# Reordering the work lists of the SSD scan groups (one tile's convolution, two products, and a separate list for the last group)

## The reference, cut to what matters

```
xbc = silu(dwconv_centred(xbc, conv_w, conv_b))          # per group: B, C and four x tiles
cb = einsum('bclgn,bcsgn->bgcls', cc, bc)
wmat = cb[:, :, None] * _segsum_exp(a_cum)               # scores of a chunk
y_diag = einsum('bghcls,bcsghp->bclghp', wmat, xd)       # product inside the chunk
states = einsum('bclgn,bclghp->cbghpn', bc, xd * decay)  # state of each chunk
y_off = einsum('bclgn,cbghpn->bclghp', cc, h_prev) * decay_out
y = rmsnorm((y_diag + y_off + xs * d_skip) * silu(z), gnorm_w);  out = y @ w_out
```

## Time and profile before

| | us |
|---|---|
| median of 3 runs (lowest, highest) | 1253.02 (1252.13, 1253.27) |
| profiled execution: its own time | 1253.8 |
| its span, first to last instruction | 1252.1 |
| TensorE busy in the span | 1154.5 (92%) |
| VectorE busy | 876.2 (70%) |
| ScalarE busy | 616.6 (49%) |
| granted TensorE clock, mean | 0.973 |

### The profile page before, as it was taken

One profiled execution on the slowest core, in us unless ns is written; L12 is line 12 of the kernel. 1 busy time (PEld: TensorE's weight loads), 2 busy tenths in 40 slices (PEclk: granted clock), 3 DMA queues, 4 the chain that ended last, 5 costly groups with the idle time before them and its releaser, 6 DMA issues.

```text
span 1252.1 us, 20419 instructions
## 1 busy us (share of the span) xinstructions
PE 1154.5 (92%) x7420; PEld 693.7 (55%) x7420; DVE 876.2 (70%) x1385; ACT 616.6 (49%) x1100; POOL 86.8 (7%) x102
## 2 busy tenths in 40 slices
PE   3999899998987999899999999997898996999996
PEld 2545444454444447644444444475555585888886
DVE  5695877768677976677878779735466767655654
ACT  4676565656566433633333332225454464566642
POOL 0004013040320000000000000000000000000000
PEclk9999999999997999899999999999999998999998
DMA  9423130221313253246464636421322114355552
GB/s 387 160 76 127 68 135 33 81 86 67 135 68 136 77 216 143 81 176 233 175 233 175 230 135 242 170 98 68 119 75 76 61 42 168 135 201 201 193 187 91
DMA packets 24535, 174.07 MB, mean 139 GB/s; under 512 B 2720, under 2 KB 2720, under 8 KB 5536
## 3 DMA queue, kind: packets, MB, share of 16 engines
q1 hardware_dynamic: 18432, 128.24, 28.2%
q0 software_dynamic: 4608, 33.56, 7.5%
q10 hardware_dynamic: 1440, 11.53, 2.5%
HBM read 172.27 MB, written 1.05 MB: 138 GB/s over the span
## 4 chain that ended last, share of the span: by engine, by line
PE 77%; DVE 12%; ACT 6%; issue 4%; DMA 1%; DVEq 0%; ACTq 0%; SPq 0%
PE bank L1726 21%; PE bank L1728 20%; PE bank L1727 20%; ACT wh L428 2%; PE bank L1900 2%; DVE wl L963 2%; DVE sq L1142 1%; PE bank L2175 1%; PE bank L1930 1%; PE bank L2189 1%; PE bank L1941 1%; ACT arena L535 1%; PE bank L1915 1%; ACT arena L470 1%; DVE arena L1225 1%
## 5 line engine op out<-in xcount | busy, mean ns | idle before, releaser
L1726 PE MATMUL bank<-hh,wh 128*128 128x512 f16 (+1 forms) x1168 | 396.7, 340 | 13.9 <-DVE hl L1032 5.3
L1727 PE MATMUL bank<-hl,wh 128*128 128x512 f16 (+1 forms) x1168 | 396.2, 339 | 0.0
L1728 PE MATMUL bank<-hh,wl 128*128 128x512 f16 (+1 forms) x1168 | 396.0, 339 | 0.0
L963 DVE SCALAR_TENSOR_TENSOR wl<-raw,wh 128x1024 f16<-128x1024 f32 x224 | 270.2, 1221 | 176.1 <-ACT wh L428 174.5
L428 ACT ACTIVATE wh<-raw 128x1024 f16<-128x1024 f32 x224 | 229.0, 1041 | 252.6 <-PE bank L1728 203.5
L1726 PE MATMUL bank<-arena,wh 128*128 128x256 f16 (+1 forms) x620 | 194.2, 313 | 6.8 <-DVE arena L1472 2.8
L1728 PE MATMUL bank<-arena,wl 128*128 128x256 f16 (+1 forms) x620 | 194.0, 313 | 0.0
L1727 PE MATMUL bank<-arena,wh 128*128 128x256 f16 (+1 forms) x620 | 194.0, 313 | 0.0
L1726 PEld LDWEIGHTS bank<-hh,wh 128*128 128x128 f16 x1168 | 115.7, 99 | 114.4 <-issue 30.9
L1728 PEld LDWEIGHTS bank<-hh,wl 128*128 128x128 f16 x1168 | 115.5, 99 | 89.0 <-issue 2.7
L1727 PEld LDWEIGHTS bank<-hl,wh 128*128 128x128 f16 x1168 | 115.5, 99 | 81.4 <-issue 10.0
(11 more groups left out here) (261 smaller groups left out, 1336.9 us busy)
## 6 DMA issues: line engine op xcount, KB each, us to landing
raw<-wgu SPq DMA_DIRECT2D x44, 1024.0 KB, 4.7
arena<-wadaT POOLq DMA_DIRECT2D x32, 1024.0 KB, 5.0
raw<-wdn SPq DMA_DIRECT2D x16, 896.0 KB, 4.8
raw<-wxg SPq DMA_DIRECT2D x12, 1024.0 KB, 5.0
arena<-wada SPq DMA_DIRECT2D x8, 1024.0 KB, 19.2
raw<-wz SPq DMA_DIRECT2D x8, 1024.0 KB, 4.7
araw<-wada ACTq DMA_DIRECT2D x8, 1024.0 KB, 4.8
raw<-wout SPq DMA_DIRECT2D x8, 1024.0 KB, 5.9
```

The lines of the kernel that those rows point to most:

```text
L963: ve.scalar_tensor_tensor(wl[:, u.slot, a:b], raw[:, u.slot, a:b], WS, wh[:, u.slot, a:b], ALU.mult, ALU.subtract).then_inc(lo_done, 1)
L1726: pe.matmul(o, wh[:, u.slot, wsl], ahi[:, k, a:e], start=st, stop=False)
L1727: pe.matmul(o, wh[:, u.slot, wsl], alo[:, k, a:e], start=False, stop=False)
L1728: i = pe.matmul(o, wl[:, u.slot, wsl], ahi[:, k, a:e], start=False, stop=en)
```

## The change

```diff
@@ ScalarE
+            def silu_ahead():
+                act.activation(small[:, 60:61], eps, ACT.Silu)
@@ group(g, u)
                 tap(g + 1, 3)
+                exps(g, 2, 0)
+                exps(g, 2, 1)
                 cvt(u.plus(3))
-                for q in range(4):
-                    exps(g, 2, q)
+                exps(g, 2, 2)
+                exps(g, 2, 3)
                 silu_xbc(g + 1, 0)
                 silu_xbc(g + 1, 1)
-                silu_xbc(g + 1, 2)
-                silu_xbc(g + 1, 3)
                 evac_pre(u.plus(2), g + 1, 4, 0)
                 evac_pre(u.plus(2), g + 1, 5, 1)
                 tap(g + 1, 4)
                 tap(g + 1, 5)
+                exps(g, 3, 0)
+                exps(g, 3, 1)
                 cvt(u.plus(4))
-                for q in range(4):
-                    exps(g, 3, q)
+                exps(g, 3, 2)
+                exps(g, 3, 3)
+                silu_xbc(g + 1, 2)
+                silu_xbc(g + 1, 3)
                 silu_xbc(g + 1, 4)
@@ last_group(g, u), from square_z(0) on
                 square_z(0)
+                silu_ahead()
                 z_out(u)
                 ada_parts(g)
                 act.dma_start(araw[:, :], crow).then_inc(crow_in, 16)
                 cvt(u.plus(2))
-                square_z(1)
                 for q in range(4):
                     exps(g, 1, q)
-                for q in range(3):
-                    exps(g, 2, q)
+                square_z(1)
+                exps(g, 2, 0)
+                exps(g, 2, 1)
                 act.wait_ge(gl_ok, 2)
+                silu_ahead()
                 z_out(u.plus(1))
+                exps(g, 2, 2)
+                exps(g, 2, 3)
                 square_z(2)
                 cvt(u.plus(3))
-                exps(g, 2, 3)
+                for q in range(3):
+                    exps(g, 3, q)
                 square_z(3)
-                exps(g, 3, 0)
-                exps(g, 3, 1)
+                exps(g, 3, 3)
                 act.wait_ge(gl_ok, 4)
                 square_z(4)
                 act.wait_ge(gz_ok, 1)
                 act.activation(sqA, G[:, 12:16, 0:TC], ACT.Square).then_inc(sqd, 4)
-                exps(g, 3, 2)
-                exps(g, 3, 3)
@@ VectorE, gate_part
-                ve.wait_ge(yb_ok, (NG - 1) * NCH + c + 2)
+                if c == NCH - 1:
+                    ve.wait_ge(yb_ok, NG * NCH + 1)
+                else:
+                    ve.wait_ge(a_free, (NG - 1) * A_PER + (A_YT[c] + 2))
@@ group(g, u)
                 add_state(g, 3)
+                conv_tile(g + 1, 1)
                 add_state(g, 4)
@@
                 off(g, 0)
                 half_chunk(g, 1, 1)
-                conv_tile(g + 1, 1)
+                off(g, 1)
                 state_second(g, 0)
-                off(g, 1)
                 chunk_first(g, 1)
                 conv_tile(g + 1, 2)
                 state_second(g, 1)
                 half_chunk(g, 2, 0)
                 cvt(u.plus(3))
                 off(g, 2)
+                half_chunk(g, 2, 1)
                 conv_tile(g + 1, 3)
-                half_chunk(g, 2, 1)
                 chunk_first(g, 2)
                 state_second(g, 2)
                 conv_tile(g + 1, 4)
+                off(g, 3)
                 half_chunk(g, 3, 0)
-                off(g, 3)
                 cvt(u.plus(4))
                 half_chunk(g, 3, 1)
@@ last_group(g, u)
+                cvt(u.plus(1))
                 x_rows(g, 0)
                 x_rows(g, 1)
-                cvt(u.plus(1))
                 half_chunk(g, 0, 0)
@@
+                cvt(u.plus(2))
                 off(g, 0)
-                cvt(u.plus(2))
                 half_chunk(g, 1, 0)
...
+                chunk_first(g, 0)
+                half_chunk(g, 1, 1)
+                off(g, 1)
+                state_second(g, 0)
+                chunk_first(g, 1)
+                state_second(g, 1)
+                add_z(1)
+                off(g, 2)
+                half_chunk(g, 2, 0)
+                gate_part(1, 0, TC)
+                gate(1)
+                half_chunk(g, 2, 1)
+                add_z(2)
+                chunk_first(g, 2)
+                state_second(g, 2)
+                gate_part(2, TC, TC + P)
+                half_chunk(g, 3, 0)
+                off(g, 3)
+                add_z(3)
+                half_chunk(g, 3, 1)
+                add_z(4)
+                add_part()
+                from_state(g, 3)
+                cvt(u.plus(3))
                 from_chunk(g, 3)
@@ TensorE, hooks of a looped group, units 2 and 3
-                              3: lambda: (within(2, 0), exponents(2, 3)),
-                              4: lambda: from_states(2),
+                              3: lambda: (from_states(2), exponents(2, 3)),
+                              4: lambda: within(2, 0),
                               6: lambda: y_turn(2),
                               7: lambda: (within(2, 1), exp_pair(3))},
                              {0: lambda: from_states(3),
-                              1: lambda: exponents(3, 2),
-                              2: lambda: within(3, 0),
-                              3: lambda: (y_turn(3), exponents(3, 3)),
+                              2: lambda: exponents(3, 2),
+                              3: lambda: exponents(3, 3),
+                              4: lambda: (y_turn(3), within(3, 0)),
                               6: lambda: within(3, 1),
                               7: lambda: b_and_cb(g + 1)}]
@@ the last group: four tables and the formula are replaced by three tables
+                    hooks = [{0: lambda: exp_pair(0),
+                              1: lambda: (x_turn(0), x_turn(1)),
+                              2: lambda: ada_part(g, 0),
+                              3: lambda: (exponents(0, 2), x_turn(2), x_turn(3), exponents(0, 3)),
+                              4: lambda: state(0),
+                              5: lambda: state(1),
+                              6: lambda: (within(0, 0), state(2)),
+                              7: lambda: (ada_part(g, 1), state(3))},
+                             {0: lambda: (within(0, 1), state(4)),
+                              1: lambda: (exp_pair(1), state(5)),
+                              2: lambda: (ada_turn(g), from_states(0)),
+                              3: lambda: exponents(1, 2),
+                              4: lambda: (within(1, 0), exponents(1, 3), from_states(1)),
+                              5: lambda: y_turn(0),
+                              6: lambda: (within(1, 1), exp_pair(2)),
+                              7: lambda: (y_turn(1), from_states(2))},
+                             {1: lambda: exponents(2, 2),
+                              2: lambda: (within(2, 0), exponents(2, 3)),
+                              3: lambda: y_turn(2),
+                              4: lambda: (exp_pair(3), from_states(3)),
+                              5: lambda: (within(2, 1), exponents(3, 2)),
+                              6: lambda: exponents(3, 3),
+                              7: lambda: (within(3, 0), y_turn(3), within(3, 1))}]
```

More of the change, by code:

```diff
@@ L1342, in last_group @@
                 ada_out(g)
+                cvt(u.plus(2))
                 off(g, 0)
-                cvt(u.plus(2))
                 half_chunk(g, 1, 0)
-                from_state(g, 0)
-                from_chunk(g, 0)
+                chunk_first(g, 0)
[4 more added lines that the diff above has]
+                state_second(g, 1)
                 add_z(1)
-                off(g, 1)
-                half_chunk(g, 1, 1)
-                from_state(g, 1)
+                off(g, 2)
                 half_chunk(g, 2, 0)
-                from_chunk(g, 1)
-                off(g, 2)
                 gate_part(1, 0, TC)
                 gate(1)
+                half_chunk(g, 2, 1)
                 add_z(2)
-                half_chunk(g, 2, 1)
-                from_state(g, 2)
+                chunk_first(g, 2)
[3 more added lines that the diff above has]
+                off(g, 3)
                 add_z(3)
-                from_chunk(g, 2)
-                gate_part(2, TC, TC + P)
+                half_chunk(g, 3, 1)
+                add_z(4)
+                add_part()
+                from_state(g, 3)
                 cvt(u.plus(3))
-                half_chunk(g, 3, 0)
-                add_z(4)
-                off(g, 3)
-                add_part()
-                half_chunk(g, 3, 1)
-                from_state(g, 3)
                 from_chunk(g, 3)
@@ L1988, in group @@
                 else:
-                    hooks = [{1: lambda: exp_pair(0),
-                              2: lambda: (x_turn(0), x_turn(1)),
-                              3: lambda: ada_part(g, 0),
-                              4: lambda: (x_turn(2), x_turn(3), exponents(0, 2)),
-                              5: lambda: state(0),
-                              6: lambda: (state(1), exponents(0, 3)),
```

(30 more changed lines are left out.)

## The result

The changed kernel takes 1232.21 us (median of 4 runs, 1231.34 to 1233.63), the kernel before 1253.14 (4 runs beside them, 1252.13 to 1253.74). The ratio is 0.9836 (95% interval 0.9823 to 0.9849; intervals stand in brackets from here on), a gain of 20.5 us by the ratio and 20.9 by the two medians. The forecast was 1231.3. The profiled execution took 1231.34 us with a span of 1229.5, against 1253.8 and 1252.1.

A forecast was written before the change was run, and what follows sets the result against it. TensorE was taken as the bound, losing time to the order of VectorE's list. Loop 16.2, group 0's low clock 1.7 and last group 3.9 sum to 21.8 us, off 1253.8; with the median 0.8 lower, forecast 1231.3 us, range 1226 to 1242.

The forecast's parts named there:

- The loop: Looped groups of the scan: four TensorE stalls of 5.4 us a group go, 16.2 us in three groups.
- the walk: Reckoned times of instructions and TensorE slots in the new lists; smallest margin in the looped groups 1.1 us.
- part 2: Unit 2 of a looped group: stalls of 2.07 and 1.68 us before `within(2, 0)` and `within(2, 1)` go.
- part 3: Unit 3 of a looped group: stalls of 0.71 and 0.94 us go, the first before `exponents(3, 2)`.
- Part 1: Early in a looped group: tile 1's convolution moves between two `add_state`, taking 3.0 to 4.75 us; cost 0.
- rival C: Moved convolution: each step waits for one GpSimd instruction, 3.1 us more, `from_states(0)` stalls 1.3 a group; 1235.2 us, chance 0.13.
- E: Slower: the moved convolution is one long obstacle, at 13 us losing 8.3 a group; 1256 us, chance 0.06.
- Group 0's low clock: Group 0 of the loop: the 3.4 us at 1.2 GHz after the first stall goes, 1.7 us.
- The last group: Last group, first step to sum of squares: VectorE's closing list ends at 396.8 instead of 400.75, gaining 3.9 us.
- Rival B: The loop gains but the last group doesn't; 1235.1 us, or 1237 with it 2 us worse; chance 0.20.
- D: Looped groups: stalls move as margins before `within(3, 1)` and `within(3, 0)` fail; 1241 us with half kept; chance 0.11.

The follow-up runs named there:

- e4: Changed kernel with TensorE's list in the looped groups put back as before; 1241.61 us, ratio 0.9921.
- e6: Changed kernel with VectorE's list in the looped groups put back as before; 1239.73 us, ratio 0.9897.
- e5: Changed kernel with ScalarE's list in the looped groups put back as before; 1237.5 us, ratio 0.9886.
- e3: Changed kernel with tile 1's convolution put back behind `half_chunk(1, 1)` in the looped groups; 1234.37 us, ratio 0.9854.
- e11: The kernel before itself, no edit, run again for a second profile; a single run, 1249.86 us.
- e8: The changed kernel itself, no edit, timed again; 1232.6 us, ratio 0.9843.
- e2: Kernel before with only the last group changed, looped groups as before; 1249.67 us, ratio 0.9978.
- e1: Kernel before with only the looped groups changed on all engines, last group as before; 1233.63 us, ratio 0.9857.
- e10: Kernel before with only the looped groups changed, run once more with more rounds; 1235.05 us, ratio 0.9852.

## Why the prediction was right, step by step

The time lies 0.9 us from the forecast, and the greatest term, the loop, came by the forecast mechanism. The nearness of the whole is in part luck: two terms were read from one execution of the kernel before and aren't in every one, and 1.0 us came from behind the scan that no term had.

**The loop** (16.2 forecast, 16.8 measured). Right in mechanism and size. The losses read from start to start summed to 5.4; the brackets alone would have given 5.0, and 5.61 came. All four stalls went, none came in their place, and the four slots fell within 0.2 us of the walk. e4 to e6 show that the steps named on each engine were the ones that mattered: the stall of e5 at `evac_pre` of tile 4 and the 0.39 at `exponents(3, 2)` are those that part 2 and part 3 said the moved silus and exponentials take away.

**Part 1** (0 forecast, no stall measured, one reason false). `from_states(0)` runs at 195.59 in the changed kernel with no bracket, and the price of the convolution, 4.38 us, lies inside the range of 3.0 to 4.75 but far from the 3.0 that I reckoned with. GpSimd beside it in group 1:

```profile
189.61 1.48 POOL L1688 TENSOR_TENSOR arena<-arena 128x512 f32<-128x512 f32 x1 [1.23 <-DVE arena L1267]
191.07 3.98 POOL L1701 TENSOR_SCALAR arena<-arena 128x512 f32<-128x512 f32 x4
```

Against rival C I had argued that VectorE keeps its time under xD and xD alone grows. Here both grew: the four steps of the convolution from 3.11 us to 4.38, by 1.27, xD from 2.71 to 3.98, the decay from 1.04 to 1.48. In e3, where this convolution isn't beside them, the three take 3.11, 2.69 and 1.04 again. The Trainium skill, "SBUF — State Buffer", Who interferes with whom, has such a pair exclude each other, one fully blocked until the other is done. The trace agrees that they slow each other, and shows less than C's full sum: 1.27 us in place of 3.1, and no step of the scan over the 1.42 us of the source view below (minimum, median and maximum in ns). That longest step began at 190.22, 0.87 us before the decay's listed end; had it stood still until then it would have taken 0.87 + 0.75 = 1.62 (listed spans of GpSimd are rough).

```profile
L1152 DVE SCALAR_TENSOR_TENSOR arena<-arena,small x36: 739/905/1415, 114.9 to 303.2; 128x512 f32<-128x512 f32 x36
```

C and E, which lived on this price, are refuted for this kernel, with 0.6 us of room: the end of the last `add_state` here is 195.0, and the product that waits for it starts at 195.59; in e3 the room is 1.3. e3 adds what the prediction didn't ask: without the move only 0.4 us a group would be lost, so the move of the convolution is the smallest part of the gain.

**Group 0's low clock** (1.7). Present in the profiled execution that the sum was made against, and gone in the changed kernel. e11 shows that it isn't in every run of the kernel before. As a term against that one execution it was right; as a term of the median it was luck.

**The last group** (3.9 forecast, 3.45 measured, 0.3 where neither spell of low clock falls). The walk of the new list was good. In the coordinates of the kernel before (18.16 added), VectorE's closing list started at 377.7 and ended at 397.25; the walk had 376.9 and 396.8. `state(0)` finds its rows, `within(1, 0)` waits 1.49 us (0.8), the first step of unit 2 0.59 (0.7), and TensorE has nothing to do for some 10 us. The 0.8 left out `chunk_first(0)`: the trace ends that wait with L1204, which takes 0.68 us behind `half_chunk(1, 0)` and frees the product's bank. This is most of the 0.8 us by which VectorE's closing list starts later than walked. The mis-sized thing is the other side of the subtraction: 78.6 us, taken from one execution, held 3.2 us that the same list loses to low clock only in some runs (75.45 to 78.64 in four passes; the new list has 75.15 to 75.20 in those of the changed kernel, e8 and e2). What the new list does beyond 0.3 us is take away the wait of 1.95 us in front of `state(0)`, after which the clock falls in some runs (1.7 us), and the spell ahead of the last score product (up to 1.5 us). The timed value of the new last group is 2.8 us on the old loop (e2), and 1.0 to 2.8 on the new one (e1, e10 against the changed kernel's 1232.2 to 1232.6), where the intervals of the ratios overlap. Rival B, "the last group gains nothing", had 1235.1; the kernels without the new last group take 1233.6 and 1235.05, and the changed one 1232.2. So B is refuted by e2, but the last group's gain is less than the 3.9 forecast, and as a term of the median 3.9 was too much by 1 us or more.

**D** (the stalls move) is refuted by the empty timeline. The margins of 1.1 and 1.5 us held; e3 shows that a further 3 us of VectorE's work ahead of them would have cost only 0.4.

**Not foreseen:** 1.0 us of the span from behind the scan, whose cause isn't shown; the 2 us in the range cover it.

## What to carry to other kernels

Walk each engine's list in slots, in one set of coordinates, and read the loss of a stall from start to start instead of from its bracket; with that, this reordering over three engines was forecast to 0.2 us a pass. Include the instruction that frees a product's bank, not only the one that makes its operand. Take the terms that hang on the clock from more than one execution: the same wait is followed by a fall in one and not in the next. Where the clock stays low until the same moment, as at the end of this scan, matmuls that start earlier give back half of what was gained (2.1 us became 1.0); work for TensorE in the wait recovered some of it.

## What the runs showed of the hardware

- One wait of 1.95 us at the same place of the same list: followed by a granted clock of 0.66 or 0.73 in a window of 5 us in two passes, and by 1.00 in two others. The fall costs 1.7 us each time (25.80 us for 24.11).
- Another spell of 3.4 us at 1.2 GHz in the same list cost 0.07 us (e11), because TensorE would have waited 1.30 us for VectorE behind it without the spell (e1).
- With 47 idle matmuls in the waits the mean clock over 24 us was 0.86 in place of 0.51. The median was 2.8 us lower, in another set; 1.6 us of it is seen in the traces. Whether fewer than 47 would do wasn't tried.
- VectorE's convolution steps beside GpSimd took 4.38 us for four, where they take 3.11 alone (e3); GpSimd's xD took 3.98 for 2.71. The loss is shared, 1.27 us each. What sets its size in a given place stays open.
